# Softmax attention on Trainium2: scores of two pairs of heads in PSUM, transposed weights in rounds of four blocks, one maximum for both heads

## What is computed

```python
def attend(q, k, v):
    s = jnp.einsum('btgrd,blgd->bgrtl', q, k, preferred_element_type=jnp.float32) * (ATTN_HEAD_DIM ** -0.5)
    p = jax.nn.softmax(s, axis=-1)
    return jnp.einsum('bgrtl,blgd->btgrd', p.astype(v.dtype), v)
```

## Time and profile before

| | |
|---|---|
| median of 3 runs | 3650.16 us (3645.24 to 3651.47) |
| the profiled execution | 3644.49 us, of which the span of the trace is 3642.7 |
| granted TensorE clock over the span | 0.938 |
| PE busy | 3301.4 us, 91% |
| DVE busy | 1872.5 us, 51% |
| ACT busy | 1172.0 us, 32% |
| POOL busy | 180.8 us, 5% |
| window read as the first attention stage | 1251.2 to 1422.1 us |
| as the second | 2405.1 to 2530.7 us |
| as the third | 3297.0 to 3396.1 us |

### The profile page before, as it was taken

How to read it: one execution, slowest core, us unless ns; L and a number is a source line. 1 busy time by engine, 2 the same in 40 slices (tenths; PEclk the granted TensorE clock), 3 DMA queues, 4 the chain that set the end, 5 groups by cost and what they waited for, 6 DMA issues and landing times.

```text
span 3642.7 us, 44475 instructions
## 1 busy us (share of the span) xinstructions
PE 3301.4 (91%) x18616; PEld 2722.9 (75%) x18616; DVE 1872.5 (51%) x2747; ACT 1172.0 (32%) x1764; POOL 180.8 (5%) x136
## 2 busy tenths in 40 slices
PE   8899878999998888899989899988999798998997
PEld 8777567888886766677767788866888676775776
DVE  2852444665544475677644543556534444456544
ACT  3212333122123254422234333234212343434322
POOL 0000000000001000000000320000000002100000
PEclk9998789999998999999999999998989799999998
DMA  4541001333321100355431122200212212220231
GB/s 173 155 134 41 1 24 58 126 123 123 126 81 59 53 1 30 117 178 179 150 109 60 64 77 89 73 22 28 88 62 86 79 58 84 91 95 18 84 98 58
DMA packets 88108, 305.91 MB, mean 84 GB/s; under 512 B 9570, under 2 KB 11491, under 8 KB 87397
## 3 DMA queue, kind: packets, MB, share of 16 engines
q1 hardware_dynamic: 81060, 285.76, 23.9%
q10 hardware_dynamic: 6848, 17.30, 1.3%
HBM read 281.53 MB, written 21.50 MB: 83 GB/s over the span
## 4 chain that ended last, share of the span: by engine, by line
PE 76%; DVE 10%; ACT 8%; issue 4%; DMA 1%; POOL 0%; ACTq 0%; POOLq 0%; DVEq 0%; SPq 0%
PE PS L382 75%; ACT whi L193 2%; PE PS L385 1%; DVE JUNK L489 1%; DVE stage L489 1%; ACT Pq L1223 1%; DVE STs L1260 1%; ACT nt L586 1%; DVE wlo L207 1%; DVE STq L1260 1%; ACT Ps L1223 1%; ACT U L591 0%; DMA stage<-in_ada 0%; DVE fg L689 0%; ACT Ht L2253 0%
## 5 line engine op out<-in xcount | busy, mean ns | idle before, releaser
L382 PE MATMUL PS<-U,whi 128*128 128x512 f32 (+1 forms) x5408 | 1174.1, 363 | 91.2 <-DVE U L611 25.3
L382 PEld LDWEIGHTS PS<-U,whi 128*128 128x128 f32 x5408 | 910.1, 192 | 280.3 <-issue 56.8
L207 DVE TENSOR_TENSOR wlo<-stage,whi 128x1024 fp32r<-128x1024 f32 x339 | 414.9, 1225 | 1107.3 <-ACT whi L193 1106.6
L193 ACT ACTIVATE whi<-stage 128x1024 fp32r<-128x1024 f32 x339 | 358.5, 1058 | 1529.4 <-PE PS L382 1464.4
L382 PE MATMUL PS<-U,wlo 128*128 128x512 f32 (+1 forms) x2704 | 619.0, 355 | 0.0
L382 PE MATMUL PS<-Y,whi 128*128 128x512 f32 (+1 forms) x2240 | 581.8, 363 | 18.3 <-DVE Y L691 12.3
L382 PEld LDWEIGHTS PS<-U,wlo 128*128 128x128 f32 x2704 | 457.0, 189 | 79.5
L382 PEld LDWEIGHTS PS<-Y,whi 128*128 128x128 f32 x2240 | 396.4, 190 | 93.3 <-DVE Y L691 14.2
L382 PE MATMUL PS<-Y,wlo 128*128 128x512 f32 (+1 forms) x1120 | 367.4, 362 | 0.0
L382 PE MATMUL PS<-whi,U 128*128 128x512 f32 (+2 forms) x832 | 224.4, 360 | 25.0 <-ACT mQK L866 11.3
L382 PEld LDWEIGHTS PS<-Y,wlo 128*128 128x128 f32 x1120 | 208.7, 190 | 34.8
(11 more groups left out here) (416 smaller groups left out, 3415.1 us busy)
## 6 DMA issues: line engine op xcount, KB each, us to landing
stage<-in_w SPq DMA_DIRECT2D x128, 512.0 KB, 3.3
stage<-in_ada SPq DMA_DIRECT2D x80, 512.0 KB, 3.3
stage<-in_adb SPq DMA_DIRECT2D x48, 512.0 KB, 3.3
stage<-in_p_mg SPq DMA_DIRECT2D x16, 512.0 KB, 3.3
stage<-in_p_ma SPq DMA_DIRECT2D x16, 512.0 KB, 3.5
stage<-in_p_ms SPq DMA_DIRECT2D x16, 512.0 KB, 3.5
stage<-in_wo SPq DMA_DIRECT2D x16, 512.0 KB, 3.3
GS<-FS ACTq DMA_DIRECT2D x20, 384.0 KB, 2.4
```

The costliest lines, as they stand in the source:

```text
L193: act.activation(self.parts[r % n][0], self.stage[i % len(self.stage)], ACT.Copy).then_inc(*self.S.up("w_hi", i))
L207: dve.tensor_tensor(lo, self.stage[i % len(self.stage)], hi.bitcast(F32), ALU.subtract).then_inc(*self.S.up("w_lo", i))
L382: return pe.matmul(o, l, r, start=start, stop=stop_, skip_group_check=True)
```

## The change

Scores of a job lie in three banks in place of four: head 0 from the first column, head 1 so that it ends with the third bank. For 512 columns or fewer the middle bank is unused; for more, both heads have their columns above 512 in it, and the last score matmul of a job waits by a semaphore (`a_mid`) for the first. Two jobs fit (banks 0 to 2 and 3 to 5), so the scores of n+1 wait no more for the exponentials of n. The matmuls of a job are put in pairs of unlike width and written in two halves. Both masks of a job of 640 columns become one matmul for each head. The transposes are written in rounds of four blocks of 128 columns, the two heads in turn, all in one bank (6); each round is copied by ACT to PT before the next, so a job of 768 columns has three rounds, one of 512 has two and one of 256 has one. DVE copies nothing any more. The maximum of both heads is one instruction over a view of three dimensions, and so is its negated form. The loops of the three engines are written anew, with one job more in flight.

```diff
-        A_TURN = PS[:, 2048:3072].rearrange("p (h c) -> p h c", h=2)
-        A_REST = PS[:, 3072:3584].rearrange("p (h c) -> p h c", h=2)
+            def scores(self, n):
+                k, c = B.where.get(("a_s", self.tag, n), 0), self.width(n)
+                return PS[:, k:k + 2 * (1536 - c)].rearrange("p (h s) -> p h s", s=1536 - c)[:, :, 0:c]
+
+            def pieces(self, n):
+                c, low, high = 0, [], []
...
+                        (high if c >= 512 else low).append((c, k0, m))
...
+                one = [(0, k0, m, at_) for at_, k0, m in high + low]
+                two = [(1, k0, m, 1536 - min(c, 512) + at_) for at_, k0, m in low] + [
+                    (1, k0, m, 1536 - c + at_ - 512) for at_, k0, m in high]
+                return [x for both in zip(one, two) for x in both]
+
+        A_TURN = PS[:, 3072:3584].rearrange("p (b c) -> p b c", c=128)
...
+            def scores(n, part):
+                key = ("a_s", a.tag, n)
+                if part == 0:
+                    B.claim(pe, 3 * (n % 2), 3, key, (("a_exp", a.tag, n, 0), ("a_exp", a.tag, n, 1)))
...
+                cut = len(ps) // 2
+                for i, (h, k0, m, to) in list(enumerate(ps))[cut * part:len(ps) if part else cut]:
+                    if c > 512 and i == len(ps) - 1:
+                        pe.wait_ge(*at("a_mid", a.tag, n))
...
+            def turn(i, r):
+                n_ = a.width(i) // 64
+                if r:
+                    pe.wait_ge(*at("a_pt", a.tag, i, r - 1))
...
+                if r == 0:
+                    pe.wait_ge(*at("a_p", a.tag, i, 1))
+                for x in range(4 * r, min(4 * r + 4, n_)):
+                    last = tr(pe, A_TURN[:, x - 4 * r, :], a.P[i % 2][:, x % 2, 128 * (x // 2):128 * (x // 2) + 128], 128)
...
+            for n in range(N + 3):
+                if 0 <= n - 3 < N:
+                    values(n - 3)
+                rounds = a.rounds(n - 2) if 0 <= n - 2 < N else 0
+                for r in range(3):
+                    if r < rounds:
+                        turn(n - 2, r)
+                    if r < 2 and n < N:
+                        scores(n, r)
...
+            for n in range(N + 3):
+                if 0 <= n - 3 < N and (n - 3) % 4 == 3:
+                    finish(act, (n - 3) // 4)
+                rounds = a.rounds(n - 2) if 0 <= n - 2 < N else 0
+                for r in range(3):
+                    if r < rounds:
+                        turned(n - 2, r)
+                    if r < 2 and 0 <= n - 1 < N:
+                        weights(n - 1, r)
...
+                    dve.wait_ge(*at("a_s", a.tag, i))
+                    dve.tensor_reduce(mx, a.scores(i), AX.X, ALU.max).then_inc(*up("a_max", a.tag, i))
+                    dve.wait_ge(*at("a_max", a.tag, i))
+                    if a.sink is None:
+                        dve.tensor_scalar(nm, mx, -0.125, None, ALU.mult).then_inc(*up("a_neg", a.tag, i))
...
+                if 0 <= n - 3 < N and (n - 3) % 4 == 3:
+                    finish(dve, (n - 3) // 4)
+                if 0 <= n - 1 < N:
                     dve.wait_ge(*at("a_exp", a.tag, i, 1))
```

More of the change, by code:

```diff
@@ L1160, in pe_attention @@
                 pe.wait_ge(*at(*event))
[L1161 to L1176, removed]
-                    last.then_inc(*up("a_s", a.tag, n))
[L1178 to L1198, removed]
-                            pe.wait_ge(*at("a_ptd", a.tag, i - 1))
-                    else:
-                        B.slot(pe, 2, ("a_t", a.tag))
-                    for h in range(2):
-                        pe.wait_ge(*at("a_p", a.tag, i, h))
-                        for b in range(c // 128):
-                            t = A_TURN[:, h, 128 * b:128 * b + 128] if b < 4 else A_REST[:, h, 128 * b - 512:128 * b - 384]
-                            last = tr(pe, t, a.P[i % 2][:, h, 128 * b:128 * b + 128], 128)
-                    last.then_inc(*up("a_t", a.tag, i))
@@ new lines, in values @@
+            def values(i):
+                ti, gi, j = a.jobs[i]
+                m, nb = i // 4, a.width(i) // 128
+                if i == 0:
+                    B.claim(pe, 7, 1, ("a_o", a.tag), (freed(N // 4 - 1),))
+                if j == 0 and m:
+                    pe.wait_ge(*at(*freed(m - 1)))
+                blocks = [k0 // 128 + b for k0, kn in a.tiles[ti][1] for b in range(kn // 128)]
+                for b in range(nb):
+                    if b % 2 == 0:
+                        pe.wait_ge(*at("a_pt", a.tag, i, b // 2))
+                    for h in range(2):
+                        kb = b if nb <= 4 or h == 0 else (b + 4) % nb
+                        last = mm(pe, A_OUT[64 * h:64 * h + 64, 128 * j:128 * j + 128], a.value(gi, h, blocks[kb]),
+                                  a.PT[:, 2 * b + h, :], b == 0 and j == 0, b == nb - 1)
+                last.then_inc(*up("a_o", a.tag, i))
@@ L1214, in act_attention, with weights @@
             N = len(a.jobs)
[L1215 to L1218 removed]
+            def weights(n, h):
+                mx, nm, sm, rd = a.stat(n)
+                c = a.width(n)
+                if h == 0:
                     if n >= 2:
[L1220 to L1236 removed]
@@ new lines, in weights @@
+                        act.wait_ge(*at("a_t", a.tag, n - 2, a.rounds(n - 2) - 1))
+                    act.wait_ge(*at("a_neg", a.tag, n))
+                act.activation(a.P[n % 2][:, h, 0:c], a.scores(n)[:, h, :], ACT.Exp, bias=nm[:, h:h + 1],
+                               scale=0.125, accum_out=sm[:, h:h + 1]).then_inc(*up("a_exp", a.tag, n, h))
+                if h and a.sink is not None:
+                    act.wait_ge(*at("a_off", a.tag, n))
+                    act.activation(mx, mx, ACT.Exp).then_inc(*up("a_sink", a.tag, n))
@@ L1238, in dve_attention @@
         def dve_attention(dve, a, finish):
             N = len(a.jobs)
-            for n in range(N + 2):
+            for n in range(N + 3):
                 if 0 <= n - 1 < N:
```

103 lines of the change are left out of this document (46 added, 57 removed).

## The result

| | before | after |
|---|---|---|
| median of the runs | 3650.74 us (3645.24 to 3651.47) | 3696.77 us (3693.01 to 3700.73, 4 runs) |
| ratio, 95% interval | | 1.0125 [1.011, 1.014] |
| the profiled execution, its span | 3644.49, 3642.7 us | 3696.67, 3694.9 us |
| first stage (S) | 170.9 us | 175.5 us |
| second stage (Q0) | 125.2 us | 145.6 us |

The kernel is slower by 46 us. The forecast was 3672 us, which is 22 more than the median of before (the sum behind it gave 26 to 28), and the measured median lies 0.8 us above the range. A stage's length is read from its first score matmul to its last value matmul. The three stages give +44.7 us of the 52.2 by which the spans of the two profiled executions differ; the other 7.5 lie between the stages and behind the last.

What follows compares the result with a forecast made beforehand. It took TensorE as 91% busy and the attention stages as paced by a softmax ring through DVE and ACT. S +7, Q0 and Q1 +10.6 each, the rest 0: +28, taken as +26, so 3672 us, range 3644 to 3696.

Steps and rivals of the forecast that it cites:

- The ring through DVE and ACT: Attention stages: one job's whole softmax, nothing in it overlapping, sets the pace; 5.78 us for 768 columns against 4.97.
- The maximum as the last wait: Before a job's first exponential: one maximum of both heads, 1.75 us at 768 columns, behind the previous scaling; exponential 0.28 later.
- The finish: Output finished every fourth job: its stall goes in S; in Q0 and Q1 that job takes 7.6 us against 6.77.
- The rest ... together 0: Stage starts, stage ends and the eight jobs of 256 columns cancel: together 0, from -5 to +5 us.
- second form of rival B: TensorE after idle stretches: mostly 1.2 GHz, which 0.3 to 0.9 us slack a job doesn't cover; rival B's chance 0.18.
- The starts: Start of each stage: first jobs pay TensorE's lower clock on more work ahead, +1 to +3 us each.
- The ends: End of each stage: three round trips of transposes replace one, but last values wait less, -2 to 0 us.
- TensorE's changes of shape: TensorE's work per 768-column job: three further tile-shape changes, up to 0.2 us each, make 4.9 us 5.5, under the ring.
- Rival A: Attention stages: scores run ahead and TensorE becomes the bound, about -30 us, 3615; chance 0.10.
- Rival B's first form: Score halves of unequal width don't overlap, each lasting 1.49 us; +16 us, so 3688; rival B's chance 0.18.
- The bound of 0.2%: Whole kernel: a measurement tells a difference of 0.2% (7 us) from no change; chance within it 0.08.

Runs made afterwards that it cites:

- e3: Kernel before with one maximum and one negation for both heads, banks and order of work unchanged: 3677.19 us.
- e4: Changed kernel with a maximum and a negation for each head in jobs of 512 columns or fewer: 3700.01 us.
- e10: Kernel before with only S in the order of e5, and there a maximum for each head in 512-column jobs: 3634.25 us, 0.9956.
- e5: Changed kernel with both exponentials of a job together on ACT behind the first copy, the second and third copy behind them: 3655.63 us.
- e1: Changed kernel with one 512-column score matmul done twice more in the finish loop of Q0 and Q1: 3694.84 us.
- e2: Changed kernel with ACT's part of the finish in Q0 and Q1 moved behind the exponential of head 0: 3682.91 us, 1.0077.
- e6: Changed kernel with DVE's maximum ahead of the previous job's scaling, and ACT's finish behind head 0's exponential in Q0 and Q1: 3804.79 us.
- e7: As e6, with ACT's finish moved in all stages and ACT's exponentials ahead of the copies: 3740.12 us, 1.0271.
- e11: The kernel of e5 with ACT's part of the finish in Q0 and Q1 behind the exponentials: 3668.82 us, 1.0045.

## Why the prediction was right in direction and wrong in size

- *The ring through DVE and ACT* was right. Per job 5.71 us against 5.78, 5.45 against 5.60, 4.95 against 4.98; at 768 columns the copy, at 0.47 and not 0.55, is the difference. (For the kernel before, the prediction first puts two maxima into the ring; only the first is in it, as its own list says further on.) e3 shows what the one maximum does to the kernel before by itself: +33 us in the stages. It is no share of the 44.7 here, since the ring is another one (with e4, taking 0.53 us off the maximum of 512 columns gained nothing), and for 768 columns no run has the changed kernel with the maximum split.
- *The maximum as the last wait* was true for 640 and 768 columns in the changed kernel, but incomplete. Between scaling and exponential runs a second chain, over round 0 and its copy; at 512 columns it is as long (e4, e10), and with the exponentials together it sets the pace at 768 too (e5).
- *The finish* came out at the forecast number, in part by luck: none in S, 7.3 to 8.0 us in Q against 7.6. With the clock kept up (e1) such a job takes 7.24 us. From the maximum's end to the exponential 1.85 us pass (3363.76 to 3365.61) and not 2.1, and the lower clock adds 0.4 that no term had.
- *The term that failed* is "The rest ... together 0", and with it the second form of rival B. The text named the clock ("mostly 1.2 GHz", "a slack of 0.3 to 0.9 us a job doesn't cover four microseconds at that level") and then set no price for it, with the reason that it "came about once per finish too" before. Before, TensorE had 0.49 us of slack in a job of 4.97; the granted clock fell behind five of six finishes, and yet three of the six jobs behind one took 5.0 us and three 5.75 to 6.34, so half of them did pay, but little. Now the loop is full: at the upper clock TensorE's work is 5.46 of 5.70 us. The lower level also lasts longer: 0.60 over 4 us before is 3.2 us of it, 0.66 and 0.50 over the two windows after are 6.7. The job behind a finish takes 2.1 to 2.7 us more than a steady one, six times: 14.4 us. e1 takes this away with work that has no use, e2 by removing the wait. Why the clock falls behind these waits and not behind the longer ones of e3 stays open.
- *The starts* cost +5.0 us in Q0 and +4.2 in Q1 (forecast +1 to +3), and the likely reason is the same, more work at the lower clock before the ring is running (windows of Q1 from 3336 to 3344 us show 0.50 granted); no run takes the starts apart. *The ends* gave back nothing in Q1 (8.93 us from the start of the last exponential, before 8.91), and the jobs of 256 with their end cost 1 us in Q0.
- Put together for Q1: 10.6 forecast, +6.8 behind three finishes, +4.2 for the start, -0.5 for pitches and the finish jobs, -1.5 because some jobs of before had taken longer than 4.97: +19.6, as measured. Q0 goes the same way, +20.4 with +7.6 behind its finishes, +5.0 for the start and -3.1 for jobs of before. S came 2 us under the forecast, since four jobs of 640 took 21.8 us and not 22.4. The point 3672 was itself 4 us low against its own sum: +26 was added to a base between the profiled execution (3644.5) and the median (3650.2).
- *TensorE's changes of shape* were sized well: 5.46 us of work against 4.9 without them and 5.5 with. The Trainium skill (TensorEngine Tiling, Key Properties) has each change drain the engine; the rows agree as far as they go: each of the six groups of a job takes 0.06 to 0.15 us more than its term of the 4.9, but no run separates the drain from other costs, and none shows the 0.2 us that was allowed for a change.
- *Rival A* (TensorE's work alone sets the pace) didn't come about: in the steady job the maximum has no idle time and the transposes wait for the scaling. The rule named with it, that groups rotate through banks, held as far as it goes: the scores of the next job do lie under the softmax, and it gained nothing, since they had not been the only thing in the ring. *Rival B's first form* is refuted: a half of the scores, 256 columns of one head beside 512 of the other, lasts 1.13 us and not 1.49. Its price (+16, so 3688) came near the measured 3697 by luck, since the loss lies at the finish and the start and not in every job.
- *The bound of 0.2%* for what a measurement tells was too narrow: the kernel before ran from 3638.8 to 3662.0 us on one chip.

## What to carry to other kernels

Before doubling a buffer, write down the serial chain through each engine's queue: a second buffer takes a step out of the ring only if nothing else in the queues' order holds the steps together, and an instruction moved ahead takes its wait with it and makes all behind it wait (e6, e7). Merging two instructions for two halves of the data saves a fixed cost of 0.15 us and can lose a whole overlap (0.7 us here). Where TensorE's loop nearly fills the ring, price a wait of 2 us twice: as the wait, and, as a possibility with a chance of its own, as the work behind it at half the clock (six of six here, one of six in e3, where the ring has 1.2 us of slack); put what causes it (here the finish) where the engine that is waited for has another reason to wait.

## What was not expected of the hardware

- 1.84 us of idle time on TensorE, in a loop that is otherwise full, were followed by 0.50 granted clock and a job longer by 2.1 to 2.7 us. Idle stretches of 0.54 us at a finish (e2) and 0.30 us in every job (e5) were followed by jobs at their usual 5.70 us. But the longer ones of e3 (2.77 to 3.06 us) were followed by a clock of 1.00 five times of six: the length of one wait doesn't decide.
- Work without use in the gap kept the clock up and shortened two stages by 16 us (e1).
- Once the clock had fallen, a group of projections without idle time on TensorE ran at 0.53 of it and took 29.4 us (e11; 29.3 in e1 and e2), where it took 16.2 at 1.00.
